# A table of turns built from its middle chunk: GpSimd forms the upper half, ScalarE writes the lower half as its mirror

## The reference, cut to what matters

```python
def s5_mixer(u, lam_re, lam_im, log_dt, b_re, b_im, c_re, c_im, d, w_glu, b_glu):
    ...
    lam = lax.complex(lam_re.astype(f32), lam_im.astype(f32))
    dt = jnp.exp(log_dt.astype(f32))[:, None]
    lam_bar = jnp.exp(lam * dt)
    ...
    def step(state, u_chunk):
        bu = jnp.einsum("gnp,btgp->btgn", b_bar, u_chunk.astype(jnp.complex64))
        a = jnp.broadcast_to(lam_bar, bu.shape)
        _, xs = lax.associative_scan(binop, (a, bu), axis=1)
        xs = xs + pow_t[None] * state[:, None]
        y = jnp.real(jnp.einsum("gpn,btgn->btgp", c, xs))
        return xs[:, -1], y
```

## Time and profile before

| | us |
|---|---|
| median of three runs | 2266.24 |
| the profiled execution, its own time | 2268.01 |
| its span in the trace | 2266.3 |
| TensorE busy | 2110.7 (93%) |
| VectorE busy | 1622.6 (72%) |
| ScalarE busy | 980.1 (43%) |
| GpSimd busy | 638.7 (28%) |

### The profile page before, as it was taken

One profiled execution on the slowest core, in us unless ns is written; L12 is line 12 of the kernel. 1 busy time (PEld: TensorE's weight loads), 2 busy tenths in 40 slices (PEclk: granted clock), 3 DMA queues, 4 the chain that ended last, 5 costly groups with the idle time before them and its releaser, 6 DMA issues.

```text
span 2266.3 us, 40688 instructions
## 1 busy us (share of the span) xinstructions
PE 2110.7 (93%) x13216; PEld 1807.1 (80%) x13216; DVE 1622.6 (72%) x2328; ACT 980.1 (43%) x1385; POOL 638.7 (28%) x729
## 2 busy tenths in 40 slices
PE   5999998995999999998999966979999999999997
PEld 4878876774888888887888865868888888888886
DVE  6686554765788888887776765678888888875555
ACT  4344343333444444444445422444444444444442
POOL 8962100693000000005877756430000000002221
PEclk8999999897999999999999987989999999999998
DMA  4555433352755555555777776535555555556654
GB/s 134 170 158 171 154 116 111 117 180 74 241 185 185 185 185 185 185 185 167 217 224 222 212 236 208 180 133 178 186 185 186 185 187 185 187 185 187 185 181 135
DMA packets 144180, 400.81 MB, mean 177 GB/s; under 512 B 22256, under 2 KB 42864, under 8 KB 144128
## 3 DMA queue, kind: packets, MB, share of 16 engines
q1 hardware_dynamic: 128864, 383.36, 53.0%
q10 hardware_dynamic: 15264, 16.78, 2.2%
HBM read 379.11 MB, written 20.97 MB: 177 GB/s over the span
## 4 chain that ended last, share of the span: by engine, by line
PE 62%; DVE 18%; issue 8%; POOL 8%; DVEq 2%; ACT 2%; DMA 1%; ACTq 1%; SPq 0%; POOLq 0%
PE bank L316 33%; PE bank L315 17%; DVE lo L296 6%; DVE cgv L1113 3%; PE bank L312 2%; DVE cgv L1110 2%; DVE sumt L330 2%; PE bank L1482 1%; PE bank L1484 1%; PE bank L1483 1%; POOL tab L778 1%; DVE ut L366 1%; PE bank L313 1%; DVE th L1270 1%; POOL ut L778 1%
## 5 line engine op out<-in xcount | busy, mean ns | idle before, releaser
L316 PE MATMUL bank<-xx,hi 128*128 128x512 f32 x3540 | 1271.4, 401 | 0.0
L315 PE MATMUL bank<-xx,lo 128*128 128x256 f32 x3540 | 1000.4, 283 | 5.8 <-DVE xx L1391 5.8
L296 DVE TENSOR_TENSOR lo<-raw,hi 128x1024 fp32r<-128x1024 f32 x698 | 880.4, 1293 | 140.0 <-ACT hi L289 132.0
L289 ACT ACTIVATE hi<-raw 128x1024 fp32r<-128x1024 f32 x698 | 711.7, 1053 | 343.9 <-PE bank L316 300.6
L316 PEld LDWEIGHTS bank<-xx,hi 128*128 128x128 f32 x3540 | 672.5, 190 | 154.8
L315 PEld LDWEIGHTS bank<-xx,lo 128*128 128x128 f32 x3540 | 676.4, 191 | 16.1 <-issue 6.1
L316 PE MATMUL bank<-aa,hi 128*128 128x512 f32 x1344 | 472.8, 394 | 0.0
L315 PE MATMUL bank<-aa,lo 128*128 128x256 f32 x1344 | 376.0, 280 | 3.1 <-DVE lo L296 3.1
L316 PEld LDWEIGHTS bank<-aa,hi 128*128 128x128 f32 x1344 | 252.4, 188 | 58.8
L315 PEld LDWEIGHTS bank<-aa,lo 128*128 128x128 f32 x1344 | 252.4, 188 | 5.9 <-DVE lo L296 4.3
L1113 DVE SCALAR_TENSOR_TENSOR cgv<-sumt,par,cgv 128x255 f32<-128x255 f32 x368 | 180.6, 491 | 54.4 <-DVE cgv L1113 26.1
(11 more groups left out here) (294 smaller groups left out, 1885.2 us busy)
## 6 DMA issues: line engine op xcount, KB each, us to landing
raw<-in_up SPq DMA_DIRECT2D x344, 512.0 KB, 3.9
raw<-in_down SPq DMA_DIRECT2D x160, 448.0 KB, 4.0
raw<-in_w_in SPq DMA_DIRECT2D x98, 512.0 KB, 4.0
raw<-in_w_out SPq DMA_DIRECT2D x32, 512.0 KB, 3.3
raw<-in_down SPq DMA_DIRECT2D x32, 512.0 KB, 3.5
raw<-in_glu SPq DMA_DIRECT2D x32, 512.0 KB, 3.6
s_c<-cp ACTq DMA_DIRECT2D x16, 256.0 KB, 4.4
s_p<-ut ACTq DMA_DIRECT2D x16, 256.0 KB, 4.4
```

The costliest lines, as they stand in the source:

```text
L289: A.activation(hi[:, s, :], raw[:, s, :], ACT.Copy).then_inc(hi_done, 1)
L296: V.tensor_tensor(lo[:, s, :], raw[:, s, :], hi[:, s, :].bitcast(f32), SUB).then_inc(lo_done, 1)
L315: TE.matmul(bank[:, L:], lo[:, s, w], x2[:, k, 0, :], start=False, stop=False)
L316: last = TE.matmul(bank[:, :], hi[:, s, w], x2[:, k, :, :], start=False, stop=k == total - 1)
```

## The change

The origin of the angles moves from chunk 0 to chunk 32 (`MID`). GpSimd writes chunk 32 with cosine 1 and sine 0 and doubles from there with n = 2, 4, 8 and 16, which fills chunks 32 to 63. The doubling n = 32 with its 24 instructions is gone. Chunk 0, which is 32 steps before the middle, is written from the squared unit: its cosine, and its sine with the sign changed. ScalarE writes chunks 1 to 31 as the mirror image of chunks 63 to 33: one activation copies the cosines in reverse order, the other the sines with a scale of -1. These stand behind the splits of the output projection and ahead of the norm, wait for `rot_new`, and raise `rot_whole`, for which the table's store now waits. `rot_new` is now raised after tile 3.

```diff
 C5 = L // T5
+MID = C5 // 2
...
-                c, s = rot_c[:, pr, 0:n], rot_s[:, pr, 0:n]
+                c, s = rot_c[:, pr, MID:MID + n], rot_s[:, pr, MID:MID + n]
...
-                G.tensor_tensor(rot_c[:, pr, n:2 * n], w[:, 0], w[:, 1], SUB)
-                return G.tensor_tensor(rot_s[:, pr, n:2 * n], w[:, 2], w[:, 3], ADD)
+                G.tensor_tensor(rot_c[:, pr, MID + n:MID + 2 * n], w[:, 0], w[:, 1], SUB)
+                return G.tensor_tensor(rot_s[:, pr, MID + n:MID + 2 * n], w[:, 2], w[:, 3], ADD)
...
-            G.memset(rot_c[:, :, 0], 1.0)
-            G.memset(rot_s[:, :, 0], 0.0)
+            G.memset(rot_c[:, :, MID], 1.0)
+            G.memset(rot_s[:, :, MID], 0.0)
             for part, x in enumerate((rot_c, rot_s)):
-                G.tensor_scalar(x[:, :, 1], rho[:, 1, part, :], 1.0, None, MUL)
+                G.tensor_scalar(x[:, :, MID + 1], rho[:, 1, part, :], 1.0, None, MUL)
...
                 if i == 3:
                     next_unit()
-                if i in (3, 5, 7):
-                    x = (i - 3) // 2
-                    chain(turns(32, x * PAIRS // 4, (x + 1) * PAIRS // 4))
-            turns(32, 3 * PAIRS // 4, PAIRS).then_inc(rot_new, 1)
+                    G.tensor_scalar(rot_c[:, :, 0], rho[:, 0, 0, :], 1.0, None, MUL)
+                    G.tensor_scalar(rot_s[:, :, 0], rho[:, 0, 1, :], -1.0, None, MUL).then_inc(rot_new, 1)
...
             with a.Fori(0, KT // 2) as i:
                 act_split(a, B_OUT + LEAD, 4, i, range(4))
+            a.wait_ge(rot_new, 1)
+            for x, sign in ((rot_c, 1.0), (rot_s, -1.0)):
+                ins = A.activation(x[:, :, 1:MID], x[:, :, C5 - 1:MID:-1], ACT.Copy, scale=sign)
+            ins.then_inc(rot_whole, 1)
...
-                    a.wait_ge(rot_new, 1)
+                    a.wait_ge(rot_whole, 1)
                     for part, x in enumerate((rot_c, rot_s)):
                         a.dma_start(s5_rot[:, :, part, :].rearrange("k p n -> p k n"),
```

## The result

The changed kernel takes 2246.88 us in the median (2244.48 to 2249.79), against 2265.85 us for the kernel before in the same comparison. The ratio is 0.9914, with a 95% interval from 0.9902 to 0.9926. The forecast was 2247.1 us in a range of 2244.8 to 2251.0.

What follows compares the result with a forecast made beforehand. GpSimd's queue of squares was taken to bound the output projection's end, TensorE its body. Gains of 16.86 (wait) and 2.23 us (norm), with mirror and later stages at 0, made 2266.24 - 19.1 = 2247.1 us; range 2244.8 to 2251.0.

Steps and rivals of the forecast that it cites:

- The bound: End of output projection: the norm's matmul waits for GpSimd's last sum of squares; removing three queued blocks gains 16.86 us.
- Does GpSimd catch up?: Tiles 4 to 14: GpSimd reaches the floor at 2.1 us a pair; rival of failing, up to 3.5 us, shares chance 0.15.
- the long block: Six doubling instructions on GpSimd took 9.73 us beside weight splits for 6.86 us of work, giving 2.1 us a pair.
- the mean of two consecutive pairs: Square-and-sum pairs on GpSimd beside weight splits, 2.80 us, above the 2.55 us limit; argued to be unfair.
- slack: GpSimd's spare time before the output projection's last tile, put at 2.6 us.
- The fourth quarter: Last six n = 32 instructions, beside the norm's reciprocal and first eight scalings; their removal gains 2.23 us.
- The mirror: ScalarE's two activations between last weight split and norm's root: 2.05 us each, hidden, costing nothing.
- The cover: ScalarE's idle time between its last split and the norm's root after the change, 8.4 us.
- The dear end: Mirror at the every-fourth-element gather's 3.0 ns an element: 12.0 us together, 3.6 us visible; within a rival of chance 0.15.
- The clock: TensorE's lower clock after the pause, up projection's start: 0.5 us lost, put at -1.0 to +0.8 us, nothing in the sum.
- Given back later: Rival: later stages paced by loads take back the gain; half given back makes 2256.7 us; chance 0.05.
- The sum: Whole kernel: 16.86 + 2.23 + 0 + 0 = 19.1 us gained, 0.84%, for a median of 2247.1 us.

Runs made afterwards that it cites:

- the kernel with one more quarter: Changed kernel plus six GpSimd instructions of 128x512 into spare memory behind tile 3; 2252.83 us, ratio 0.9945.
- that part alone: Kernel before, with the last six instructions of the n = 32 doubling held back until the norm's last low half is written; 2264.99 us, ratio 0.9993.
- all seven kernels of the table: The changed kernel and six variants of it or of the kernel before, whose norm matmul waited 2.65 or 2.66 us for GpSimd; medians 2246.88 to 2265.40 us.
- the forward copy: Changed kernel plus two ScalarE activations ahead of the mirror, 1984 elements read forward and 512 reading every fourth; 2247.53 us, ratio 0.9924.
- The kernels that moved the turns: Kernel before with all 24 n = 32 instructions moved behind the norm's last low half (2259.05 us) or directly behind the last sum of squares (2265.40 us).

## Why the prediction was right

- **The bound.** It was GpSimd's queue of squares, as read from the earlier trace rows. From the first product to the norm's matmul it was 524.79 - 413.31 = 111.48 us and is 504.78 - 410.25 = 94.53, a gain of 16.95 against the 16.86 predicted.
- **Does GpSimd catch up?** Tiles 4 to 13 took 496.98 - 475.01 = 21.97 us, 2.2 us a pair against 2.1 from the long block; the mean of two consecutive pairs, 2.80, was the wrong row, as argued. The prediction gave 2.6 us of slack; the idle times in GpSimd's timeline make 3.2, and the kernel with one more quarter confirms them: 6.86 - 3.2 = 3.66, measured 3.67.
- **The fourth quarter.** 2.23 us predicted, 2.16 with that part alone. The changed kernel's norm shrank by more, 13.16 - 10.41 = 2.75 us. The extra 0.52 us is a term that I missed: the norm's matmul takes 0.70 us in place of 1.22, since TensorE's granted clock, still 1.00 from 500 to 505 us, has not yet fallen when it runs after 2.65 us of idle time. It takes 0.70 us in all seven kernels of the table with that wait, and 1.22 us in all that waited 6.32 us or more, as in the second layer after 4.47 us.
- **The mirror.** Hidden, at 1.85 us each against 2.05 taken. The cover was put at 8.4 us and is 505.52 - 497.59 = 7.9, as the norm's matmul is 0.5 us shorter. The dear end, the gather's rate, was the wrong neighbour: the forward copy shows that the step of -1 costs nothing.
- **The clock.** Its 0.5 us of added loss did not come. The mean clock over the 7 us from the first product is 0.73, against 0.65 before: 3.8 us at the lower level against 4.9. A pause as short as the second layer's was not followed by a stretch as long as there.
- **Given back later.** Nothing that can be seen: the rest is 0.7 us shorter, within its scatter. The kernels that moved the turns show that it could have been otherwise, but only for work that GpSimd still does.
- **The sum.** 19.1 us predicted, 19.70 in the profiled stage, 19.0 between the medians. The mechanism and each term came as forecast, but that the median lies 0.2 us from the forecast is luck: the four runs spread over 5.3 us, and the sum lacked the 0.5 us of the norm's matmul.

## What to carry to other kernels

When a helper engine stands at the end of a stage, count its work per tile at the rate it gets beside the others, from a long stretch of its timeline; what exceeds the slack came out here one to one, at its rate alone, for instructions of the same kind. For two long copies their spans in the trace were no measure of it. Work that fills an idle engine's gap is not free if it shares SBUF reads with the engine on the path: moved behind the norm it gave back half of the gain in the profiled execution and 12.2 of 19.0 us between the medians, and removed it gave back nothing. The symmetry that halves the table paid in full here because the other half is written by an engine with a pause of its own, and the pause could be read before the change as the idle time ahead of the instruction that must not be delayed.

## What the runs showed of the hardware that I had not expected

- Continuous GpSimd reads slow VectorE's two-input instructions by a factor of three: eight scalings of 128x256 span 10.16 us in place of 3.26, and a reciprocal beside them keeps 1.75 us. In short bursts I had seen only 5.47.
- Beside VectorE's splits GpSimd takes 5.2 to 6.1 us for a one-input copy of 1984 elements in rows of 31, ScalarE 1.85 us; the read's direction matters to neither. A split that meets such a copy takes up to 4.61 us in place of 1.22.
- The same products of the output projection take up to 1.4 us longer through TensorE's clock at their start alone (a body of 92.94 us with a mean of 0.85 over the first 20 us, and of 91.49 us with 0.93).
